# First layer's second weight slot in halves, early products of ones, and gate rows spread by transfers

## What is computed

```python
x = x + 0.5 * swiglu(rmsnorm(x, g), w_in, w_out)        # first block, twice per layer, with a mixer between
# second block: shift, scale and gate come from silu(c) @ w_ada + b_ada
u = rms_norm(h, norm_pre) * (1.0 + scale) + shift
h = h + resid_w * gate * rms_norm(fn(u), norm_post)     # fn: swiglu, token mixer, swiglu
```

## Time and profile before

| | |
|---|---|
| median of 3 runs | 1601.88 us (1601.79 to 1603.11) |
| the profiled execution | 1604.88 us, its span 1603.1 us |
| PE busy | 1580.2 us (99% of the span) |
| DVE, ACT, POOL busy | 1139.3, 818.6, 66.7 us |
| bytes read from HBM | 319.62 MB, 200 GB/s over the span |

### The profile page before, as it was taken

How to read it: one execution, slowest core, us unless ns; L and a number is a source line. 1 busy time by engine, 2 the same in 40 slices (tenths; PEclk the granted TensorE clock), 3 DMA queues, 4 the chain that set the end, 5 groups by cost and what they waited for, 6 DMA issues and landing times.

```text
span 1603.1 us, 20837 instructions
## 1 busy us (share of the span) xinstructions
PE 1580.2 (99%) x7549; PEld 1305.7 (81%) x7549; DVE 1139.3 (71%) x1255; ACT 818.6 (51%) x984; POOL 66.7 (4%) x99
## 2 busy tenths in 40 slices
PE   7999999999999999999999999999999999999998
PEld 5888888888888888887888888888887888878887
DVE  5565568868777787777776878688787466775554
ACT  5455563354444544455665444554446576564443
POOL 2000100000000010000000000000000000000000
PEclk9999999999999999999999999999999999999999
DMA  7766753338888598855445988758893454446662
GB/s 238 247 195 220 241 184 110 128 132 269 276 270 271 175 304 263 281 196 174 143 130 177 294 271 273 257 195 281 269 308 130 155 171 146 162 150 218 207 217 86
DMA packets 242396, 337.25 MB, mean 210 GB/s; under 512 B 14185, under 2 KB 180290, under 8 KB 242336
## 3 DMA queue, kind: packets, MB, share of 16 engines
q1 hardware_dynamic: 196288, 281.05, 53.1%
q0 software_dynamic: 11280, 39.56, 6.7%
q10 hardware_dynamic: 34768, 15.83, 4.0%
HBM read 319.62 MB, written 1.05 MB: 200 GB/s over the span
## 4 chain that ended last, share of the span: by engine, by line
PE 94%; DVE 3%; ACT 2%; DMA 1%; issue 0%; SPq 0%; DVEq 0%; ACTq 0%
PE ps L573 27%; PE ps L575 27%; PE ps L574 27%; PE ps L624 4%; PE ps L632 2%; PE ps L873 1%; PE ps L581 1%; DVE w_lo L1850 1%; ACT w_hi L1326 1%; DMA raw<-ffn_w_in_dram 1%; PE ps L1143 0%; PE ps L1005 0%; PE ps L1031 0%; PE ps L806 0%; DVE arena L1882 0%
## 5 line engine op out<-in xcount | busy, mean ns | idle before, releaser
L1850 DVE TENSOR_TENSOR w_lo<-raw,w_hi 128x2048 fp32r<-128x2048 f32 x265 | 604.0, 2289 | 199.4 <-ACT w_hi L1326 198.4
L1326 ACT CAST w_hi<-raw 128x2048 fp32r<-128x2048 f32 x265 | 503.8, 1911 | 324.5 <-PE ps L575 291.2
L573 PE MATMUL ps<-w_hi,actT_hi 128*128 128x512 f32 x1456 | 571.9, 393 | 1.8 <-DVE w_lo L1850 0.8
L575 PE MATMUL ps<-w_hi,actT_lo 128*128 128x512 f32 x1456 | 567.0, 389 | 0.0
L574 PE MATMUL ps<-w_lo,actT_hi 128*128 128x512 f32 x1456 | 566.7, 389 | 0.0
L573 PEld LDWEIGHTS ps<-w_hi,actT_hi 128*128 128x128 f32 x1456 | 273.4, 188 | 61.5 <-issue 3.3
L575 PEld LDWEIGHTS ps<-w_hi,actT_lo 128*128 128x128 f32 x1456 | 273.3, 188 | 57.3
L574 PEld LDWEIGHTS ps<-w_lo,actT_hi 128*128 128x128 f32 x1456 | 273.5, 188 | 55.3
L573 PE MATMUL ps<-w_hi,hT_hi 128*128 128x512 f32 x480 | 187.4, 390 | 0.0
L574 PE MATMUL ps<-w_lo,hT_hi 128*128 128x512 f32 x480 | 186.9, 389 | 0.0
L575 PE MATMUL ps<-w_hi,hT_lo 128*128 128x512 f32 x480 | 186.8, 389 | 0.0
(11 more groups left out here) (276 smaller groups left out, 1146.5 us busy)
## 6 DMA issues: line engine op xcount, KB each, us to landing
raw<-ffn_w_in_dram SPq DMA_DIRECT2D x174, 512.0 KB, 5.0
raw<-ffn_w_out_dram SPq DMA_DIRECT2D x88, 512.0 KB, 4.7
arena<-w_ada_dram POOLq DMA_DIRECT2D x72, 512.0 KB, 5.2
raw<-ffn_w_gate_dram SPq DMA_DIRECT2D x44, 512.0 KB, 4.1
raw<-ffn_w_up_dram SPq DMA_DIRECT2D x44, 512.0 KB, 5.1
raw<-ffn_w_down_dram SPq DMA_DIRECT2D x44, 512.0 KB, 4.4
raw<-w_in_dram SPq DMA_DIRECT2D x40, 512.0 KB, 4.7
raw<-hg_w_in_dram SPq DMA_DIRECT2D x32, 512.0 KB, 4.9
```

Of the source, the lines that this page charges most:

```text
L573: nc.tensor.matmul(to, hi, whi, start=start, stop=False, skip_group_check=True)
L575: return nc.tensor.matmul(to, lo, whi, start=False, stop=stop, skip_group_check=True)
L1326: nc.scalar.copy(w_hi[:, s, :], raw[:, s, :]).then_inc(hi_ready[s], 1)
L1850: nc.vector.tensor_tensor(w_lo[:, s, :], raw[:, s, :], w_hi[:, s, :].bitcast(F32), ALU.subtract)\
```

## The change

Three things are done. In the first layer slot 1 is loaded, rounded and subtracted in halves as slot 0 was, with a semaphore for each half, and PE waits for the halves. POOL fills `hidden` with ones first, and PE makes five float32 products of 128 x 256 with it, then turns the vectors, then makes one more product; their result in bank 5 is not read. For the gates, `diagonal_gate` and `gate_wide_row` go: PE turns the 128 x 8 columns to 8 x 128 (`turn_gate`), ACT copies these, and POOL issues eight transfers for each gate, each of which writes one row of 128 values to all 128 partitions of `gate_row`. The first eight stand in the middle of the modulation loads, ahead of unit 60, the other sixteen behind `tm_bias`. DVE waits for the transfers in `residual`, and PE for the smaller copy. The loads of `consts` and `levels` now share a semaphore.

```diff
+WARM = 5
-        gate_diag = region(4096, KD, P)
-        last_diag = region(14336, KD, P)
+        gate_rows = region(15872, P)[0:KD, :]
@@ up_weights, on SP
-                    if st.norm == 0 and half == 0 and isinstance(c, int) and c == 0:
-                        for part, done in ((slice(0, 2), front_loaded), (slice(2, 4), raw_loaded[0])):
-                            nc.sync.dma_start(to[:, part, 0:FC], w_gate[:, part, 0:FC]).then_inc(done, 16)
-                            nc.sync.dma_start(to[:, part, FC:COLS], w_up[:, part, 0:FC]).then_inc(done, 16)
+                    if st.norm == 0 and isinstance(c, int) and c == 0:
+                        for part, done in ((0, front_loaded[s]), (2, raw_loaded[s])):
+                            kp = slice(4 * half + part, 4 * half + part + 2)
+                            nc.sync.dma_start(to[:, part:part + 2, 0:FC], w_gate[:, kp, 0:FC]).then_inc(done, 16)
+                            nc.sync.dma_start(to[:, part:part + 2, FC:COLS], w_up[:, kp, 0:FC]).then_inc(done, 16)
@@ POOL
-            nc.gpsimd.memset(eps_col, EPS).then_inc(eps_ready, 1)
+            nc.gpsimd.memset(hidden[:, 0, :], 1.0).then_inc(memsets_done, 1)
+            nc.gpsimd.memset(eps_col, EPS).then_inc(memsets_done, 1)
...
+            def load_gate_row(i):
+                pool.wait_ge(gate_copied, i + 1)
+                for k in range(KD):
+                    nc.gpsimd.dma_start(gate_row[:, k * P:(k + 1) * P], gate_rows[k:k + 1, :].unsqueeze(1).to_broadcast([1, P, P]))\
+                        .then_inc(gate_row_loaded, 16)
             for n in range(ADA_UNITS):
+                if n == ADA_IN[6] + 6:
+                    load_gate_row(0)
...
             nc.gpsimd.dma_start(tm_bias.rearrange("p h n -> p (h n)"), a["da_bias"]).then_inc(bias_loaded, 16)
+            load_gate_row(1)
+            load_gate_row(2)
@@ PE, rounded_first
-                    if st.norm == s == t == 0:
-                        pe.wait_ge(front_lo, 1)
+                    if st.norm == t == 0:
+                        pe.wait_ge(front_lo, s + 1)
...
-            def gate_wide_row(i):
-                pe.wait_ge(diag_ready, i + 1)
-                diag = last_diag if i == 2 else gate_diag
-                for k in range(KD):
-                    last = nc.tensor.matmul(ps[:, HT_BANK + k // 4, (k % 4) * P:(k % 4 + 1) * P], C["ones"],
-                                            diag[:, k, :], start=True, stop=True)
-                last.then_inc(gate_wide, 1)
+            def turn_gate(i):
+                pe.wait_ge(mod_ready, i + 1)
+                nc.tensor.transpose(ps[0:KD, HT_BANK, 0:P], mod_gate[:, i, :], ident).then_inc(gate_turned, 1)
...
+            def warm(n):
+                for _ in range(n):
+                    nc.tensor.matmul(ps[:, 5, 0:FC], hidden[:, 0, 0:P], hidden[:, 0, :], start=True, stop=True)
+            pe.wait_ge(memsets_done, 1)
+            warm(WARM)
             pe.wait_ge(head_loaded, 32)
             nc.tensor.transpose(ps[:, SMALL_BANK, 0:48], rows_a[0:48, :], ident[0:48, 0:48]).then_inc(cols_turned, 1)
+            warm(1)
@@ ACT
-            def front():
-                act.wait_ge(front_loaded, 32)
-                nc.scalar.copy(w_hi[:, 0, 0:SLOT // 2], raw[:, 0, 0:SLOT // 2]).then_inc(front_hi, 1)
...
+            def front(s):
+                act.wait_ge(front_loaded[s], 32)
+                nc.scalar.copy(w_hi[:, s, 0:SLOT // 2], raw[:, s, 0:SLOT // 2]).then_inc(front_hi, 1)
+                act.wait_ge(raw_loaded[s], 32)
+                nc.scalar.copy(w_hi[:, s, SLOT // 2:SLOT], raw[:, s, SLOT // 2:SLOT]).then_inc(hi_ready[s], 1)
...
-                    nc.scalar.copy(gate_row.rearrange("p (h n) -> p h n", h=HALF), ps[:, HT_BANK:HT_BANK + 2, :])\
-                        .then_inc(gate_row_ready, 1)
+                    nc.scalar.copy(gate_rows, ps[0:KD, HT_BANK, 0:P]).then_inc(gate_copied, 1)
...
-            act.wait_ge(eps_ready, 1)
+            act.wait_ge(memsets_done, 2)
@@ DVE
-            def diagonal_gate(i):
...
+                    dve.wait_ge(gate_row_loaded, 16 * KD * (st.result - 6 + 1))
...
-                split_lo(1, nxt.filled[1])
-                if st is not None:
+                if st is None:
+                    front(1)
+                else:
+                    split_lo(1, nxt.filled[1])
                     residual(st, 1)
...
-                        if c == 4 and st.norm in (5, 6):
-                            diagonal_gate(st.norm - 5)
```

More of the change, by code:

```diff
@@ L548, in _ @@
             nc.gpsimd.dma_start(consts[:, P:], a["consts"][:, P:]).then_inc(consts_loaded, 16)
-            nc.gpsimd.dma_start(levels_raw, a["levels"]).then_inc(levels_loaded, 16)
-            pool.wait_ge(levels_loaded, 16)
+            nc.gpsimd.dma_start(levels_raw, a["levels"]).then_inc(consts_loaded, 16)
+            pool.wait_ge(consts_loaded, 32)
             pool.wait_ge(hT_turned, 2)
@@ L619, in rounded_first @@
                     for kk in range(4):
-                        if st.norm == s == t == 0 and kk == 2:
+                        if st.norm == t == 0 and kk == 2:
                             pe.wait_ge(lo_ready[s], st.filled[s] + 1)
@@ L642, in between @@
                     if st.kind == "ffn" and st.norm >= 6:
-                        gate_wide_row(st.norm - 6)
+                        turn_gate(st.norm - 6)
                 rounded_first(st, banks[0], 0, between).then_inc(tile0_done, 1)
@@ L653, in after_second_chunk @@
                 if st.norm >= 6:
-                    pe.wait_ge(gate_row_ready, st.norm - 6 + 1)
+                    pe.wait_ge(gate_copied, st.norm - 6 + 1)
                 if st.norm in (6, 7):
@@ L756, in ffn @@
                     if nxt is not None:
-                        gate_wide_row(nxt.norm - 6)
+                        turn_gate(nxt.norm - 6)
             def chunk(st, i, b):
@@ L963, in forget_gates @@
                     pe.wait_ge(zf_split, 1)
-                    pe.wait_ge(consts_loaded, 16)
+                    pe.wait_ge(consts_loaded, 32)
                     pe.wait_ge(small_loaded, 16 * 6)
@@ L1420, in after_out @@
                     for b in range(2):
-                        if t == b == 0 and st is None:
-                            front()
+                        if t == 0 and st is None:
+                            front(b)
                         elif t == 0:
@@ L1431, in wide @@
                 if st.norm >= 6:
-                    act.wait_ge(gate_wide, st.norm - 6 + 1)
-                    nc.scalar.copy(gate_row.rearrange("p (h n) -> p h n", h=HALF), ps[:, HT_BANK:HT_BANK + 2, :])\
-                        .then_inc(gate_row_ready, 1)
+                    act.wait_ge(gate_turned, st.norm - 6 + 1)
+                    nc.scalar.copy(gate_rows, ps[0:KD, HT_BANK, 0:P]).then_inc(gate_copied, 1)
             def ffn(st):
@@ L1851, in split_lo, with front @@
                     .then_inc(lo_ready[s], 1)
-            def front():
-                for at, hi, lo in ((slice(0, SLOT // 2), front_hi, front_lo), (slice(SLOT // 2, SLOT), hi_ready[0], lo_ready[0])):
-                    dve.wait_ge(hi, 1)
-                    nc.vector.tensor_tensor(w_lo[:, 0, at], raw[:, 0, at], w_hi[:, 0, at].bitcast(F32), ALU.subtract)\
+            def front(s):
+                for at, hi, n, lo in ((slice(0, SLOT // 2), front_hi, s + 1, front_lo), (slice(SLOT // 2, SLOT), hi_ready[s], 1, lo_ready[s])):
+                    dve.wait_ge(hi, n)
+                    nc.vector.tensor_tensor(w_lo[:, s, at], raw[:, s, at], w_hi[:, s, at].bitcast(F32), ALU.subtract)\
                         .then_inc(lo, 1)
@@ L1975, in after_out @@
                 if st is None:
-                    front()
+                    front(0)
                 else:
@@ L2529, in token_mixer @@
                 rest_ya(1)
-                diagonal_gate(2)
                 dve.wait_ge(yd_sq, 2)
```

16 lines of the change are left out of this document (4 added, 12 removed).

## The result

The changed kernel takes 1622.49 us (1621.71 to 1624.30) where the kernel before took 1602.49 on the same chip: ratio 1.0124, 95% interval 1.0113 to 1.0136. It is 20 us slower, and the prediction said 5.6 us faster. The profiled execution has a span of 1622.5 us.

A forecast was written before the change was run, and what follows sets the result against it. TensorE, 94% of the chain that ended last, was taken as the bound. Gains of 3.4 (start) + 0.1 + 0.5 + 1.6 (gates) = 5.6 us took the median from 1601.88 to 1596.3 us, range 1594.5 to 1599.5.

The forecast's parts named there:

- the paragraph on the 24 transfers: POOL's gate row transfers: each 64 KB lands in 2.6 us, long before it is read, so they cost nothing.
- the slower rival: Each gate transfer runs on one DMA engine, making weights 10 us late once: 1606.3 us, chance 0.08.
- third site: Gate at 1419 us: fewer TensorE instructions let tile 1's next products start earlier; gain 1.6 us, bounds 1.2 and 1.9.
- the sum: All gains over the whole kernel added up: 5.6 us, bounds 3.4 and 6.9.
- The start: First layer, up to the second tile's products: second weight slot in halves gains 3.4 us, bounds 2.0 and 4.1.
- The clock at 11.18: First products: 2.4 GHz gains 4.0 us, 1.2 GHz 2.0 to 3.8; rival, clock down and late half: 1597.7, chance 0.18.
- The gates: Three places where one transpose replaces 16 TensorE instructions: gains 0.1, 0.5 and 1.6 us.
- First site: Gate at 1043 us: TensorE still waits for VectorE's low part at 1050.29; gain 0.1 us, bounds 0 and 0.3.
- Second site: Gate at 1223 us: next products need ScalarE's first four blocks; gain 0.5 us, bounds 0.2 and 0.6.

The follow-up runs named there:

- 128 source partitions: Changed kernel with its 24 transfers read from 128 partitions (the identity matrix in place of the gate rows): 1598.22 us, ratio 0.9972.
- one at a time: Changed kernel with GpSimd issuing the gate transfers of the first and last gate singly, some 6 or 12 us apart: 1598.02 us, ratio 0.9971.
- the start alone: Changed kernel with its gate part taken back to the kernel before; slot 1 in halves and the early products of ones stay: 1600.04 us, ratio 0.9983.
- without ones: New start less its six products of ones, gate rows by products as in the kernel before: 1601.11 us, ratio 0.9990.

## Why the prediction was wrong

**The step that failed** is the paragraph on the 24 transfers: "A transfer of the same size, 64 KB, lands in 2.6 us", and with it "nothing" for their cost. Size was the same, but the source was not: 32 partitions there, one here. (Nor are the packets equal, as the slower rival has it: 512 bytes there, 4 KB here.) Against the kernel before on their own chips, the changed kernel lost 20.0 us and the one with 128 source partitions gained 4.6, so the transfers cost 24.6 us; the two sites of the trace make 24.1 of it (6.5, and 16.2 with the 1.4 that the third site gained besides). I had also taken the cost of a transfer to be paid by its reader, 120 us later. It was paid by the transfers queued behind, of other engines, on the same 16 DMA engines. No row of before showed a transfer that reads one partition many times, so its cost should have been bounded from both sides, and the bounds put into the range.

**The slower rival** had the right sign and the right reason to look (one partition is read), but the wrong mechanism and size. It let a transfer run on one engine of 16; the rows show all 16 busy to 90% at 30 GB/s. It let weights come late by 10 us once, at one site; in fact ScalarE's own issues were held at two sites, for 11.0 and 17.8 us, which cost 6.5 and 16.2. The rule that I set against it, from the Trainium skill's page "DMA: Bandwidth & Descriptors", section "Why a DMA increments its semaphore by 16 and not by 1", is borne out as to the engines: all 16 took part. That this meant no loss was my conclusion, and it does not follow: 16 engines reading one partition share its 25 GB/s, and partitions of one group share them too.

**The rest, read from the runs without the fault:**
- The whole of it: with 128 source partitions, or one at a time, the time is 1598.2 and 1598.0, 1.9 and 1.7 above the forecast of 1596.3 and in its range. Beside these the kernel before took 1602.86 and 1603.16, so the gain was 4.6 to 5.1 us where the sum said 5.6.
- The start. In the trace the steps came earlier than predicted. Both halves of slot 1 are subtracted by 14.0 (predicted 14.8), the second tile begins at 18.56 (predicted 19 to 21, before 23.07):

```profile
7.39 1.10 PE L594 MATMUL ps<-consts_sb,arena 128*128 128x128 f32 x8 [0.28 <-DVE arena L1906]
...
10.56 0.79 PE L637 MATMUL ps<-w_hi,actT_hi 128*128 128x512 f32 x1 [2.07 <-ACT actT_hi L1361]
...
11.67 2.35 DVE L1872 TENSOR_TENSOR w_lo<-raw,w_hi 128x1024 fp32r<-128x1024 f32 x2
...
15.56 1.91 ACT L1342 CAST w_hi<-raw 128x2048 fp32r<-128x2048 f32 x1 [0.70 <-DMA raw<-ffn_w_in_dram]
...
17.38 2.17 ACT L1361 ACTIVATE actT_hi<-ps,cols 128x128 fp32r<-128x128 f32 x8
...
18.56 0.50 PE L637 MATMUL ps<-w_hi,actT_hi 128*128 128x512 f32 x1
```

  The medians give 2.8 us for the start alone (predicted 3.4, bounds 2.0 and 4.1). The two traces are one execution each, and that of before lies 2.4 us above the median of its kernel, so I trust the medians.
- The clock at 11.18, left open in the prediction, went both ways: eight products at 1.2 GHz in the changed kernel (granted 0.57 from 10 to 14), none in the start alone; of the twelve traces with ones it fell there in three. The second tile began at 18.56 and at 18.08, so it mattered little: with the clock up, TensorE waits for ScalarE, 0.88 us for the first tile's last blocks and 0.23 us at 18.08, and with the clock down these waits are gone.
- The gates, 2.2 us predicted: 1.8 by the medians (1600.04 to 1598.22, with overlapping intervals), by another way. First site nothing, as said, though the wait of 0.15 grew to 0.90. Third site 1.4 (predicted 1.6): from the transposes to the low products of tile 1 it took 6.01 us instead of 7.29, and the wait of 0.16 is gone. Second site: about right in the changed kernel (6.93 us instead of 7.29, predicted 0.5 less), wrong by the fallen clock in four other runs.

## What to carry to other kernels

Before you take a transfer's time from another of the same size, compare how many partitions both sides touch: a row that is spread from one partition is read again for every receiver, and 512 KB of such reads held all DMA engines for 21 us. A slow transfer is paid for by what is queued behind it, also behind other engines' issues, so look at who issues next, not only at who reads the result. If only few partitions can be read, it matters which: eight rows out of one group took 23 us, out of eight groups 9. Two remedies worked about equally well, each row in 16 partitions (1599.25 us) and transfers spaced out in time (1598.02).

## What I had not expected of the hardware

- One partition gave 25 GB/s, and eight transfers in a row out of partitions 0 to 7 gave no more (21.1 and 21.2 us for 512 KB), whether in 128 packets of 4 KB or in 1024 of 512 bytes (21.4 us, on ScalarE's queue).
- An issue can be held. Four issues that take 2.52 us took 17.77 and 20.52, and the engine that issues does nothing else meanwhile.
- With the 16 products of ones gone from the second site, two waits of 1.05 us stood 1.2 us of work apart in nine traces. TensorE's granted clock fell behind them in four (0.60 to 0.65 from 1220 to 1224) and stayed at 1.00 in five; in the five traces with the 16 products or eight transposes there it stayed at 1.00. That fits a use of products whose result was needed anyway, but does not show it.
- In the changed kernel the granted clock also fell, to 0.57 at 10 to 14 us and to 0.66 at 293 to 298, in the start alone at neither place. What decides that was not found. Nor does the granted clock tell all: without ones the products from 10.22 stood 0.43 us apart, 1.2 GHz, behind an engine that had hardly worked, and the granted clock of 10 to 14 was 1.00.
